# Split sums, joint decays and quarter scores in linear attention, and a joined break in local attention

## What is computed

```python
def gla_mixer(q, k, v, lr, w_lr2, b_lr2, norm_g):          # linear attention, chunks of C = 64
    g = log_sigmoid(lr @ w_lr2 + b_lr2) / 16
    b = cumsum(g, within a chunk)                            # "cum": sums up to a row, and after it
    q_dec, k_inv = q * 64 ** -0.5 * exp(b), k * exp(-b)
    a = where(causal, q_dec @ k_inv.T, 0)                    # "a": scores inside a chunk of 64
    u = (k * exp(b_last - b)).T @ v                          # "us"
    decay = exp(b_last)                                      # "dec": one number per channel and chunk
    S = decay * S + u                                        # carried over the chunks
    o = a @ v + q_dec @ S_prev                               # "o"; then rms_norm, gate

def swa_mixer(q, k, v, q_g, k_g, sinks, slopes):            # local attention, window 128, 4 heads
    p = softmax_with_sink(q @ [k_prev, k].T - slope * distance)
    o = p @ [v_prev, v]                                      # "pv"
```

## Time and profile before

| what | value |
|---|---|
| median of 3 runs | 1904.22 us (1902.99 to 1910.22) |
| profiled execution, its own time | 1899.43 us |
| its span | 1897.6 us |
| PE busy | 1882.3 us, 99% of the span |
| POOL busy | 925.2 us, 49% |
| DVE busy | 694.0 us, 37% |
| ACT busy | 495.9 us, 26% |
| granted TensorE clock | 1.0 |

### The profile page before, as it was taken

How to read it: one execution, slowest core, us unless ns; L and a number is a source line. 1 busy time by engine, 2 the same in 40 slices (tenths; PEclk the granted TensorE clock), 3 DMA queues, 4 the chain that set the end, 5 groups by cost and what they waited for, 6 DMA issues and landing times. The chain is left out here.

```text
span 1897.6 us, 25485 instructions
## 1 busy us (share of the span) xinstructions
PE 1882.3 (99%) x10696; PEld 1539.0 (81%) x10696; DVE 694.0 (37%) x1182; ACT 495.9 (26%) x955; POOL 925.2 (49%) x868
## 2 busy tenths in 40 slices
PE   8999999999999999999999999999999999999999
PEld 6888888788888888778878887887888888887787
DVE  7556214122111343543544571141221114335442
ACT  6102113113222443322311021131122224433220
POOL 6465444444555544445455644444445454444454
PEclk9999999999999999999999999999999999999999
DMA  7565554545555556455765654445455565564556
GB/s 256 153 191 175 149 152 135 160 141 168 166 174 169 164 156 222 134 162 171 235 214 167 190 175 146 145 138 161 145 170 165 159 179 171 149 227 134 156 178 199
DMA packets 93969, 322.70 MB, mean 170 GB/s; under 512 B 10046, under 2 KB 10656, under 8 KB 93856
## 3 DMA queue, kind: packets, MB, share of 16 engines
q0 software_dynamic: 40320, 146.82, 26.9%
q1 hardware_dynamic: 43888, 155.60, 26.1%
q10 hardware_dynamic: 9648, 18.67, 2.7%
HBM read 312.66 MB, written 8.39 MB: 169 GB/s over the span
## 5 line engine op out<-in xcount | busy, mean ns | idle before, releaser
L474 POOL TENSOR_TENSOR w_lo<-w_raw,w_hi 128x512 fp32r<-128x512 f32 x576 | 762.5, 1324 | 675.1 <-DMA w_hi<-in_wstream 497.6
L513 PE MATMUL acc<-w_hi,actT_hi 128*128 128x512 f32 x1408 | 565.3, 402 | 1.1 <-ACT slots L979 1.1
L513 PE MATMUL acc<-w_hi,actT_lo 128*128 128x512 f32 x1408 | 549.4, 390 | 0.0
L513 PE MATMUL acc<-w_lo,actT_hi 128*128 128x512 f32 x1408 | 548.8, 390 | 0.0
L513 PE MATMUL acc<-actT_hi,w_hi 128*128 128x512 f32 x896 | 361.8, 404 | 9.5 <-DVE actT_lo L1377 7.8
L513 PE MATMUL acc<-actT_hi,w_lo 128*128 128x512 f32 x896 | 350.6, 391 | 0.0
L513 PE MATMUL acc<-actT_lo,w_hi 128*128 128x512 f32 x896 | 349.9, 390 | 0.0
L513 PEld LDWEIGHTS acc<-w_hi,actT_hi 128*128 128x128 f32 x1408 | 264.6, 188 | 58.3 <-issue 5.4
L513 PEld LDWEIGHTS acc<-w_hi,actT_lo 128*128 128x128 f32 x1408 | 264.3, 188 | 56.7
L513 PEld LDWEIGHTS acc<-w_lo,actT_hi 128*128 128x128 f32 x1408 | 264.9, 188 | 50.0
L454 POOL DMA_DIRECT2D w_hi<-in_wstream x280 | 159.2, 568 | 286.8 <-PE acc L513 278.0
(11 more groups left out here) (247 smaller groups left out, 1656.4 us busy)
## 6 DMA issues: line engine op xcount, KB each, us to landing
w_raw<-in_wstream SPq DMA_DIRECT2D x288, 512.0 KB, 4.5
w_hi<-in_wstream POOLq DMA_DIRECT2D x280, 512.0 KB, 3.9
out_x<-slots ACTq DMA_DIRECT2D x7, 1024.0 KB, 7.7
slots<-in_x ACTq DMA_DIRECT2D x1, 4096.0 KB, 17.4
slots<-out_x ACTq DMA_DIRECT2D x1, 4096.0 KB, 20.1
slots<-in_x SPq DMA_DIRECT2D x3, 1024.0 KB, 11.2
out_x<-slots ACTq DMA_DIRECT2D x4, 256.0 KB, 2.1
cf_sb<-in_cf ACTq DMA_DIRECT2D x1, 997.0 KB, 10.7
```

The source lines that it names most:

```text
L474: pool.tensor_tensor(w_lo[:, n % RING], w_raw[:, g % RAW, k], w_hi[:, g % HI, k].bitcast(F32), ALU.subtract).then_inc(w_ready, 1)
L513: last = nc.tensor.matmul(acc[b][:, :], lhsT, rhs, start=(k == 0 and i == 0), stop=(k == kts - 1 and i == 2))
```

## The change

Four edits on the mixers' work in `gla` and `swa`:

1. cum: DVE copies G to an fp32r tile GH and writes the rest G - GH to GL. The two triangular matrices are copied to fp32r once per layer. The two fp32 matmuls of 256 columns become four fp32r ones. The new tiles lie in `ws_hl`, and POOL's next write to it waits for the last cum.
2. dec: four fp32 matmuls of one column become two of two columns.
3. a: four score matmuls (64 x 128 by 128 columns) become eight of 64 x 64 by 64 columns, only the two diagonal blocks of 64.
4. swa: pv of tile t - 1 moves into the break of tr of tile t; 13 stages instead of 14.

```diff
-GLA_DVE = "g qd ki ke at0 at1 s00 s01 s10 s11 g3 redo y0 y1 y2 y3".split()
-SWA_PE = "tr s0 s1 pt0 pt1 pv".split()
+GLA_DVE = "g gh gl qd ki ke at0 at1 s00 s01 s10 s11 g3 redo y0 y1 y2 y3".split()
+def swa_pe():
+    out = []
+    for t in T:
+        out += ([f"{t-1}.pv"] if t else []) + [f"{t}.{x}" for x in "tr s0 s1 pt0 pt1".split()]
+    return out + [f"{TILES-1}.pv"]
...
+                 GH=ws_hl[:, 0:256], GL=ws_hl[:, 256:512], UPTO=ws_hl[:, 512:640], AFTER=ws_hl[:, 640:768],
...
                     pool.wait_ge(S_PE.sem, S_PE.at(l - 1, "small"))
+                    pool.wait_ge(A_PE.sem, A_PE.at(l - 1, f"{TILES-1}.cum"))
...
-                pe.wait_ge(A_DVE.sem, A_DVE.at(l, f"{t}.g"))
-                nc.tensor.matmul(mix[0][:, 0:256], upto, V["G"], start=True, stop=True)
-                nc.tensor.matmul(mix[0][:, 256:512], after, V["G"], start=True, stop=True) \
-                    .then_inc(A_PE.sem, A_PE.one(f"{t}.cum"))
+                pe.wait_ge(A_DVE.sem, A_DVE.at(l, f"{t}.gl"))
+                for i, m in enumerate((V["UPTO"], V["AFTER"])):
+                    for part in ("GH", "GL"):
+                        last = nc.tensor.matmul(mix[0][:, 256 * i:256 * i + 256], m, V[part],
+                                                start=(part == "GH"), stop=(part == "GL"))
+                last.then_inc(A_PE.sem, A_PE.one(f"{t}.cum"))
                 for p in range(2):
-                    for j in range(2):
-                        last = nc.tensor.matmul(mix[1][:, 2 * p + j:2 * p + j + 1], V["G"][:, p * P:p * P + P],
-                                                half[:, j:j + 1], start=True, stop=True)
+                    last = nc.tensor.matmul(mix[1][:, 2 * p:2 * p + 2], V["G"][:, p * P:p * P + P],
+                                            half[:, 0:2], start=True, stop=True)
...
                 pe.wait_ge(A_ACT.sem, A_ACT.at(l, f"{t}.qkT"))
-                for h in H:
-                    b, p = slice(DK * (h % 2), DK * (h % 2) + DK), h // 2
-                    last = nc.tensor.matmul(mh[3 - h % 2][:, h], V["QKT"][b, 256 + P * p:256 + P * p + P],
-                                            V["QKT"][b, P * p:P * p + P], start=True, stop=True)
+                plain()
+                for p in range(2):
+                    for j in range(2):
+                        for i in range(2):
+                            r, c = slice(CH * j, CH * j + CH), slice(P * p + CH * j, P * p + CH * j + CH)
+                            b, h = slice(DK * i, DK * i + DK), 2 * p + i
+                            last = nc.tensor.matmul(mh[3 - i][r, h, r], V["QKT"][b, 256 + c.start:256 + c.stop],
+                                                    V["QKT"][b, c], start=True, stop=True)
...
             def swa(l, t):
-                yield
+                def values(t):
+                    n = min(t, 1) + 1
+                    pe.wait_ge(B_ACT.sem, B_ACT.at(l, f"{t}.PT0"))
+                    pe.wait_ge(B_DVE.sem, B_DVE.at(l, f"{t}.PT1"))
+                    for h in H:
+                        for m in range(n):
+                            last = nc.tensor.matmul(mh[2][:, h], W["PT"][:, h, P * m:P * m + P],
+                                                    kv[:, t + 1 - n + m, 256 + (h // 2) * HD:256 + (h // 2) * HD + HD],
+                                                    start=(m == 0), stop=(m == n - 1))
+                    last.then_inc(B_PE.sem, B_PE.one(f"{t}.pv"))
                 if t:
-                    pe.wait_ge(B_ACT.sem, B_ACT.at(l, f"{t-1}.PT0"))
-                    pe.wait_ge(B_DVE.sem, B_DVE.at(l, f"{t-1}.PT1"))
+                    values(t - 1)
                 else:
+                    yield
...
                 yield
-                pe.wait_ge(B_ACT.sem, B_ACT.at(l, f"{t}.PT0"))
...
-                last.then_inc(B_PE.sem, B_PE.one(f"{t}.pv"))
                 yield
+                if t == TILES - 1:
+                    values(t)
...
-                    project(l, 12 + i, (12 + i) * KT, KT, 0, mixer=both(), stages=14, skip=(2, 0)[i],
+                    project(l, 12 + i, (12 + i) * KT, KT, 0, mixer=both(), stages=(13, 13)[i], skip=(2, 0)[i],
...
+                dve.tensor_copy(V["UPTO"], upto).then_inc(A_DVE.sem, A_DVE.one("upto"))
+                dve.tensor_copy(V["AFTER"], after).then_inc(A_DVE.sem, A_DVE.one("after"))
...
                     dve.scalar_tensor_tensor(V["G"], mix[1][:, 0:256], 0.0, V["T0"], ALU.min, ALU.subtract) \
                         .then_inc(*s("g"))
+                    w(A_DVE, "g")
+                    dve.tensor_copy(V["GH"], V["G"]).then_inc(*s("gh"))
+                    w(A_DVE, "gh")
+                    dve.tensor_tensor(V["GL"], V["G"], V["GH"].bitcast(F32), ALU.subtract).then_inc(*s("gl"))
```

More of the change, by code:

```diff
@@ L374, in hybrid_trunk @@
         A_ACT = Steps(sem("gla_act"), names("", T, GLA_ACT))
-        A_DVE = Steps(sem("gla_dve"), ["zero_s", "zero_a"] + names("", T, GLA_DVE))
-        B_PE = Steps(sem("swa_pe"), names("", T, SWA_PE))
+        A_DVE = Steps(sem("gla_dve"), ["zero_s", "zero_a", "upto", "after"] + names("", T, GLA_DVE))
+        B_PE = Steps(sem("swa_pe"), swa_pe())
         B_ACT = Steps(sem("swa_act"), names("", T, SWA_ACT))
```

## The result

| | before | after |
|---|---|---|
| median, same session | 1903.31 us (1899.86 to 1910.22, 7 runs) | 1891.2 us (1889.39 to 1896.65, 7 runs) |
| ratio, 95% interval | | 0.9947 (0.9936 to 0.9959) |
| profiled execution, own time | 1899.43 us | 1889.94 us |
| its span | 1897.6 us | 1887.8 us |

The forecast was 1893.7 us, or a ratio of 0.9945. The measured gain is 0.53% (0.41 to 0.64): clear of no change, with the 0.5% that the prediction took for the least that can be told inside its interval. The two medians by themselves lie 12.1 us apart (0.9936), the two profiled executions 9.5, so the times alone size the gain to some 2 us.

The account below looks back on a forecast made before the run. PE's queue, 99% busy, was taken as the bound. Savings of 3.0 + 3.5 + 3.2 + 1.4 + 0.1 less 0.7 gave 10.5 us, so 1904.2 us was forecast to become 1893.7 us, range 1888.5 to 1900.5.

Parts of the forecast that it names:

- cum, 3.0 us: Cum matmuls, 8 breaks: four fp32r at 0.12 us each, 0.48 instead of 0.86, saving 3.0 us (-0.5 to 3.4).
- fp32r at 256 columns is no cheaper: Rival on the cum matmuls: they gain nothing or lose 0.4 us; 7.0 to 7.5 saved, 1896.9 us; chance 12%.
- dec, 3.5 us: Decay matmuls, 8 breaks: two columns cost what one does, four instructions go, 0.44 us each, 3.5 us saved.
- a, 3.2 us: Score matmuls, 8 breaks: fewer rounds and no size-change pause save 0.40 us each, 3.2 us (2.0 to 3.4).
- `plain()` at nothing: Sequencer increment added ahead of the scores: put at no cost; if it drains the array, the pause stays.
- quarter scores don't save: Rival on the scores: pause stays or rounds don't overlap; they gain 1 us or less, 1896 us; chance 9%.
- swa, 1.4 + 0.1 us: Local attention: tr of tile 0 no longer waits for DVE, 1.4 us; six joined pv and tr breaks, 0.1 us.
- tr of tile 1: Local attention: its wait for L1704 was forecast covered by 0.3 us; a miss costs at most some 0.5 us, twice.
- gl, -0.7 us: DVE chain ahead of cum: 0.05 us lost in each of seven tiles, 0.35 in the second layer's tile 3.
- cum waits for gl: Rival on the DVE chain: gl 0.3 us or more late in each tile; 8 saved or less, 1896 us; 15%.
- Slower, DVE loses twice: Rival: POOL's subtractions turn gl away twice, cum starts 3.6 us late in each of 8 tiles; 1922 us; 3%.

Follow-up runs that it names:

- cum_only: Only the split sums (GH, GL, four fp32r matmuls) put on the kernel before; ratio 0.9988, median 1899.16 us.
- spread_only: The kernel before with spread 1.0 instead of 0.95 for the first local attention chunk, nothing joined, still 14 stages; ratio 0.9999.
- a_only: Only the quarter scores put on the kernel before; ratio 0.9991, median 1899.73 us.
- a_all_quarters: The changed kernel with all four 64 x 64 blocks of each head's scores computed, 32 quarter instructions; a and us break 1.277 us, no whole time given.
- gl_twice: The changed kernel with the GL subtraction done twice in a row into the same tile; one run took 1893.77 us.
- gl_psum: The changed kernel with G also written to PSUM by one more DVE operation, so the GL subtraction reads one input there; ratio 0.9938.

## Why the prediction was right

- **cum, 3.0 us.** Right. Without gl's stall a tile costs 0.393 less (1.776 - 0.936 - 0.447 for dec); forecast 0.38. The whole break, first start to next projection matmul, takes 0.93 with the stall and 0.84 without it, where the prediction looked for 0.85. The four fp32r matmuls of 256 columns start at 0.12 steps (446.49, .61, .73), except the one behind the late load, 0.21. The choice between 0.11 and 0.23 by the half of a 512-column step was the right reading. The rival *fp32r at 256 columns is no cheaper* would have cum_only at no gain, and is refuted.

The Trainium skill's rule in "TensorE: Matmul & The Clock Gate", section "The mechanism", that a load overlaps a running matmul only if its row group differs, does not hold here: all four take the full array, and a load with its stream in turn (0.11 and 0.12) could not start every 0.12. The same section also lets a load for the "background weight buffer" be pulled ahead, which these starts agree with and the prediction didn't weigh.
- **dec, 3.5 us.** Right: 3.57. Two columns pass in the 0.112 of one.
- **a, 3.2 us.** Right: 3.27. Its parts were forecast as 0.24 for rounds, 0.09 to 0.11 for the pause and 0.05 for us; the runs give 0.23 and 0.18, the 0.18 being the pause and us together. `plain()` at nothing was right too. The rival *quarter scores don't save* falls.
- **swa, 1.4 + 0.1 us.** Right: 1.41 and 0.12, and spread_only shows which edit earns which. The wait that the moved slot covers isn't the same in each execution: in a_only, where the slot is the old one, the break cost 1.381 in the first layer and 1.994 in the second. tr of tile 1, which the forecast had free by 0.3 us, had more room. Timeline of DVE and PE there:

```profile
653.51 0.69 DVE L1729 TENSOR_TENSOR slots<-slots,stat 128x512 f32<-128x512 f32 x1 [3.11 <-ACT stat L1239]
654.12 0.42 DVE L1730 TENSOR_TENSOR slots<-slots,stat 128x256 f32<-128x256 f32 x1
...
655.27 1.05 PE L770 MATMUL mix<-slots 128*128 128x128 f32 x8
...
656.16 0.60 PE L783 MATMUL mix<-cf_sb,slots 128*128 128x128 f32 x4
```

L1730, which tr waits for (L1704 before), is done at 654.54, 1.6 us ahead of tr. L1729 took 0.69 where it (as L1703) had met POOL and taken 1.96 before: with its slot it moved out of POOL's way, and that is 1.3 us of room which the forecast didn't count. It paid nothing here, as the wait was covered already.

- **gl, -0.7 us.** The total is right by luck, as the terms are off both ways. In seven tiles gl ends 0.28 behind the subtraction, as read from the earlier trace rows, and is 2.03 long (forecast some 1.9, though its own start and end give 2.01). The stall is 0.085 a tile and not 0.05: 0.6 us, forecast 0.35. For the second layer's tile 3 the forecast charged another 0.35, and nothing was lost. That was a misreading, and not a late DMA. The earlier trace rows have the second subtraction of the pair only; the trace of before has these two ahead of it:

```profile
1535.43 1.29 POOL L474 TENSOR_TENSOR w_lo<-w_raw,w_hi 128x512 fp32r<-128x512 f32 x1 [2.39 <-DMA w_hi<-in_wstream]
1536.65 0.57 POOL L454 DMA_DIRECT2D w_hi<-in_wstream  x1
```

  G is done there at 1535.65, so gl would start at about 1536.0, inside the first subtraction and ahead of the issue. Held as L1660 was in the earlier trace rows, it would end at about 1537.0 (1536.72 and 0.28), 0.9 ahead of the load's time. That is an estimate; the trace of a_all_quarters has the case itself:

```profile
1530.85 1.40 POOL L484 TENSOR_TENSOR w_lo<-w_raw,w_hi 128x512 fp32r<-128x512 f32 x1 [2.58 <-PE acc L523]
1531.14 1.39 DVE L1685 TENSOR_TENSOR ws_hl<-slots,ws_hl 128x256 fp32r<-128x256 f32 x1
...
1533.23 0.64 PE L705 MATMUL mix<-ws_hl 128*128 128x256 f32 x4
```

  gl is held to 1532.53, 0.28 behind the subtraction, and cum starts 0.7 later without a stall. In every kernel here that has gl, this tile's break is without one (0.936, and 1.382 in cum_only, where the decays aren't joined). The rival *cum waits for gl*, 0.3 or more per tile, falls; that the load waited 0.25 us and PE lost only 0.085 is the hiding that the step counted on.
- **Slower, DVE loses twice.** It didn't: gl was held once, by the pair of issue and subtraction. gl_twice shows that the edge is real, though: the first 0.46 us more on this chain cost 0.46 per tile, in full.

What hung on the reading of the earlier trace rows was the rule for who waits. gl came ahead of the subtraction by 0.44 us and lost, in seven tiles of eight; where no issue was under way it came first by 0.11 and won. The issue's record alone, which ends at 444.59, can't explain it: gl was held till 446.21, behind the subtraction. The Trainium skill, "SBUF — State Buffer", section "Who interferes with whom", has first come first served for two SBUF inputs on DVE and a GpSimd reader. The trace agrees where POOL had no issue under way, and not where it had; with one input in PSUM there is no conflict, as the page states and gl_psum shows.

That an issue under way makes the difference was not tried by itself, but the traces of the twelve kernels show it. Taken were all of DVE's TENSOR_TENSOR and SCALAR_TENSOR_TENSOR steps that begin inside an issue, or that begin with none under way and, undisturbed, would still run when the next subtraction starts. Held means that the step ends only behind the end of that subtraction.

| a DVE step's inputs, and when it begins | steps | held |
|---|---|---|
| SBUF only, 0.114 us or more into an issue | 432 | 432 |
| SBUF only, in the first 0.113 us of an issue | 53 | 2 |
| SBUF only, ahead of a subtraction, no issue under way | 841 | 13 |
| one in PSUM, inside an issue | 250 | 0 |

The 13 began at most 0.05 us ahead of the subtraction; 8 others of the 841, all near the kernel's start, took 0.2 us longer. So a step of these kinds that reads only SBUF is safe ahead of an issue and in its first 0.1 us, and late behind that. How the issue keeps a place for the subtraction behind it stays open.

## What to carry to other kernels

Where one engine's in-order queue is 99% of the time, add up its breaks start to start in the trace: here that sum told 10.5 us of gain, part by part, where the timing of a single part could hardly tell it from nothing. A short operation on such a queue is worth its form as well as its work: keep to one tile size within a break, pad partial rows where zeros are free (the breaks showed that gain, the time didn't), and take two columns where one costs a weight load. Before a DVE step is put on a path, look at what POOL is doing when it would start, in all rows and not only the last ahead of the deadline, and give one of its inputs a place in PSUM if both would come from SBUF.

## What the runs showed of the hardware that was not expected

- A DVE subtraction of two SBUF inputs that starts 0.16 us into a DMA issue of POOL's (0.57 long) ends only 0.28 behind the end of POOL's *next* instruction: 2.03 us instead of 0.42. With one input in PSUM it takes 0.42, though it starts inside the issue (0.50 into it) and runs on into the subtraction. Over all traces, 432 of 432 such steps that began 0.114 us or more into an issue were held, and 51 of 53 that began earlier in it passed.
- fp32 matmuls of 49 rows cost 0.836 us in a break, and the same over 128 rows, with zeros in those added to one operand, 0.443 to 0.449 (one 0.500).
- A change of tile size costs time without work: 0.18 us in the a break, where 64 x 128 and then 64 x 64 matmuls stood between full ones, and now 64 x 64 alone.
- fp32r matmuls of 256 columns, each with its weight load, start every 0.117 us, so the load (0.112 where it is all there is) and the stream overlap; one fp32 column and two cost the same 0.112.
